# A trunk layer with sparse attention on one core: the column sums, the query norm, the gated convolution and some top-k rounds stand at other places

## The chip, the cores and the metric

One core of one Trainium2 chip. The metric is the device time of one launch in microseconds; a launch computes the whole layer once. All arithmetic is in float32 or in products split into float32r parts.

## What is computed

```python
x = x + 0.5 * swiglu(rmsnorm(x, ffn1_norm), ffn1_w_gate, ffn1_w_up, ffn1_w_down)
h = rmsnorm(x, mix_norm)
gb, gc, xv, q, k, v, qi, ki, wi = split(h @ w_in)
u = gc * xv                                   # gated convolution, width 3, 512 channels
conv_out = gb * sum(up[:, j:j + T] * conv_w[j] for j in range(3))
q = rope_partial(rmsnorm(q, q_norm), pos, 16)  # per head of 64
k = rope_partial(rmsnorm(k, k_norm), pos, 16)
score = sum over 8 heads of relu(qi . ki) * wi # indexer; masked by chunk
sel = top_k(score, n_sel)                      # 128 keys of a stream, 68 of a running one
attn = softmax(q . k[sel] / 8) @ v[sel]
x = x + concat(conv_out, attn) @ w_out
x = x + 0.5 * swiglu(rmsnorm(x, ffn2_norm), ffn2_w_gate, ffn2_w_up, ffn2_w_down)
```

There are 640 tokens (a prompt of 512 and 8 running streams of 16 with 256 cached keys each), 1024 model columns, 2816 hidden columns, 8 query heads, 2 key heads and 8 indexer heads of 64.

## The kernel before, in words

The program is written by hand for five engines; each engine runs its own list in program order, and semaphores tie the lists. There is no scheduler: the order of the work around the change is the order of the statements.

**Split products.** PE multiplies in float32r. Every operand is a high part (`wh`, `xh`) that ScalarE copies (line 934, `mixer_hi`, `set_hi_of`) and a low rest (`wl`, `xl`) that VectorE subtracts (line 1287, `split_lo`, `mixer_lo`; line 1404, `set_rest`; line 1391, `operand_rest`). A product of a 128x128 weight tile with 640 tokens is six matmuls (lines 488, 490, 492). A *part* below is such a group of six. Raw weights come by DMA from the SP queue in units of 1 MB, two slots in turn.

**The two feed-forward stages** (`ffn(0)`, `ffn(1)`). The first unit of weights is worked in four quarters: columns 0 to 3 and 4 to 7, each with two outputs (`m`). The norm's sums of squares come beside it: ScalarE squares a tile of `x`, VectorE adds it into `sqacc` (line 1310), PE sums `sqacc` over the partitions (`column_sums`, line 499), VectorE and GpSimd make the root, VectorE writes diagonals, and PE spreads them (`broadcast_rstd`, lines 506 and 507) for ScalarE to copy into `rbc`. VectorE then scales `x` and evacuates the units (`plain_out`, `plain_hid`). After four plain units come the *sets*: a scheme of seven products in the place of eight, whose first one (`set_unit` with `first=True`) waits for `operand_rest` and `set_rest` on VectorE and for `snapshot` copies on ScalarE.

**The mixer.** Units `U_TOK` to `U_TOK + 5` make the token-major projections (queries, keys, indexer), `tok_out` copies them out. `U_CONV` to `U_CONV + 5` make the twelve outputs `proj(0)` to `proj(11)` of the convolution's gates, evacuated by VectorE's `proj_out`. `top_rounds(t, n)` does n rounds of `max` and `match_replace` on the scores of tile t (lines 1613 and 1614); tile 3 needs 16 rounds in all, 4 before the low part of `U_CONV`, 5 after it, 3 and 4 later. `weigh_sample(b)` (line 1749) weighs the indexer dots of running stream b, and between two streams VectorE squares and sums a tile of the queries (`squares_of`, lines 1573 and 1575). GpSimd makes the roots (line 1841). `head_scale` multiplies the queries with the root (line 1585) and with the gain (line 1586), `rotate` (lines 1559 to 1564) turns 16 columns of each head and signals `q_ready`. PE turns the queries (line 691) behind `q_ready`, and ScalarE copies them into `q_all`. GpSimd runs `conv(i)` (lines 1893 to 1909) as soon as `proj_out` has given it `conv_v`. Both `rotate` and `conv` read and write SBUF.

The statements of VectorE around the change:

```python
close_scores(2)
top_rounds(3, 4)
mixer_lo(U_CONV)
top_rounds(3, 5)
```

Of the kernel before, what the change touches and what calls it, by code (L numbers as in the profile page):

```python
# [27 lines left out]
P = 128  # L28
# [8 lines left out]
HD = 64  # L37
# [30 lines left out]
def trunk(nc, xt, gu1, dn1, gu2, dn2, wtok, wconv, wout, small, gains, kcache, vcache, ikcache,  # L68
          conv_past, tables, bf_tables, x_keep, y_out, k_out, v_out, ik_out, conv_out):
    with ExitStack() as ctx:  # L70
# [24 lines left out]
        sm = sb("sm", [P, 36])  # L95
# [34 lines left out]
        conv_v = spare[:, 5 * TOK:6 * TOK]  # L130
# [11 lines left out]
        conv_b = sb("conv_b", [P, TOK])  # L142
# [90 lines left out]
        head_rs_ready = sem("head_rs_ready")  # L233
        ki_ready = sem("ki_ready")
# [241 lines left out]
        def _(pe):  # L476
# [117 lines left out]
            def ffn(k):  # L594
# [4 lines left out]
                for part, (cs, m) in enumerate((cs, m) for cs in (range(0, 4), range(4, 8)) for m in range(2)):  # L599
# [332 lines left out]
        def _(act):  # L932
# [34 lines left out]
            def ffn(k):  # L967
# [176 lines left out]
            def turned_out(job, dst, n):  # L1144
# [7 lines left out]
                copy(dst, src).then_inc(bank_free[bank(job)], 1)  # L1152
# [81 lines left out]
            for t in range(TT):  # L1234
                tok_out(2, t)
            mixer_hi(U_CONV + 1)
# [11 lines left out]
            for t in range(TT):  # L1248
                turned_out(f"tq{t}", qt[:, :, t * P:(t + 1) * P] if t < 4 else qt_s, 4)
# [25 lines left out]
        def _(dve):  # L1275
# [62 lines left out]
            def ffn(k):  # L1338
# [237 lines left out]

            def mean_of_squares(n, at, ss_ready):
# [3 lines left out]
            def head_scale(z, n, at, g, rs_count):  # L1581
# [4 lines left out]
                link(dve.tensor_tensor(z, z, g.unsqueeze(1).unsqueeze(1).broadcast_to([P, TT, n, HD]), ALU.mult))  # L1586
# [34 lines left out]
            def proj_out(b):  # L1621
# [14 lines left out]
                elif part == 1:  # L1636
                    if i:
                        dve.wait_ge(conv_done, i)
                    dve.wait_ge(proj_evac, b)
                    dve.tensor_tensor(halves(conv_v[:, :]), src, halves(conv_g[:, :]), ALU.mult)\  # L1640
                        .then_inc(proj_evac, 1)
                else:
                    dve.tensor_tensor(halves(conv_b[:, :]), src, halves(rbc[:, :]), ALU.mult)\
# [56 lines left out]
            link(dve.tensor_scalar(gn[:, 0, :], gn[:, 0, :], -HD ** -0.5, None, ALU.mult))  # L1700
# [30 lines left out]
            top_rounds(3, 4)  # L1731
# [292 lines left out]
```

## Time and profile before

| | |
|---|---|
| median of 3 runs | 1237.31 us (1237.16 to 1240.55) |
| the profiled execution | 1239.92 us, of it 1238.1 us span |
| PE busy | 1202.1 us, 97% |
| VectorE busy | 806.0 us, 65% |
| ScalarE busy | 484.2 us, 39% |
| GpSimd busy | 288.4 us, 23% |
| granted TensorE clock, mean | 0.988 |

The span runs from the first to the last instruction; 1.8 us of the execution lie around it. PE holds the span nearly alone, so time is lost where PE waits and where its clock is below full. In the rows below a time in square brackets is how long the engine sat idle before the instruction, and behind it the instruction that ended the wait.

### The profile page before, as it was taken

The page shows a single profiled execution, that of the slowest core. Times are in us where ns is not written, and L with a number is a line of the kernel's source. Part 1 is how long each engine was busy: PE and PEld are TensorE (multiplying, and loading weights), DVE is VectorE, ACT ScalarE, POOL GpSimd, SP SyncE. Part 2 cuts the span into 40 slices and gives each one's busy share as a digit, 9 for nine tenths or more (in the row PEclk, how much of TensorE's full clock was granted, in tenths as well). Part 3 has the DMA queues.
Part 4 walks back from the last instruction along what each step waited for, and adds up shares of the span by engine and source line. Part 5 has one row for each costly group of instructions (what it writes and reads, how often), then busy time and mean ns, then how long its engine had stood idle before and what let it go on. Part 6 is the DMA issues. An engine that isn't in the chain of part 4 may idle for free.

```text
span 1238.1 us, 20665 instructions
## 1 busy us (share of the span) xinstructions
PE 1202.1 (97%) x7992; PEld 1156.0 (93%) x7992; DVE 806.0 (65%) x1051; ACT 484.2 (39%) x716; POOL 288.4 (23%) x217
## 2 busy tenths in 40 slices
PE   8999999999999999989899899999999999999998
PEld 7999999999999999857899679999899999999998
DVE  5898777775435452377998754678877777633433
ACT  5354444444324343341133452424444444423231
POOL 0144545450000000003663000013545454100000
PEclk8999999999999999999999899999999999999999
DMA  6112121212332233111310021420122212133222
GB/s 245 69 35 100 71 102 68 102 68 69 120 118 69 83 114 103 68 35 38 134 68 35 1 63 45 146 100 35 68 102 68 102 68 102 53 126 110 84 69 102
DMA packets 24068, 103.82 MB, mean 84 GB/s; under 512 B 3536, under 2 KB 4944, under 8 KB 16592
## 3 DMA queue, kind: packets, MB, share of 16 engines
q1 hardware_dynamic: 23136, 99.28, 22.8%
q10 hardware_dynamic: 880, 3.82, 1.0%
q8 instruction: 36, 0.59, 0.2%
q14 instruction: 16, 0.13, 0.0%
HBM read 96.99 MB, written 6.10 MB: 83 GB/s over the span
## 4 chain that ended last, share of the span: by engine, by line
PE 83%; DVE 10%; issue 3%; ACT 2%; DMA 1%; ACTq 0%; DVEq 0%
PE ps L488 13%; PE ps L490 13%; PE ps L492 13%; PE ps L526 11%; PE ps L527 11%; PE ps L528 11%; PE ps L479 2%; PE ps L481 2%; PE ps L480 2%; PE ps L691 2%; PE ps L814 1%; DVE wl L1404 1%; DVE wl L1287 1%; DVE sqacc L1310 1%; PE ps L700 1%
## 5 line engine op out<-in xcount | busy, mean ns | idle before, releaser
L934 ACT ACTIVATE wh<-raw 128x1024 fp32r<-128x1024 f32 (+3 forms) x185 | 191.7, 1036 | 398.8 <-PE ps L492 286.7
L526 PE MATMUL ps<-xs,wh 128*128 128x320 f32 x720 | 223.5, 310 | 4.9 <-DVE wl L1404 4.9
L528 PE MATMUL ps<-xs,wl 128*128 128x320 f32 x720 | 223.1, 310 | 0.0
L527 PE MATMUL ps<-xs,wh 128*128 128x320 f32 x720 | 223.1, 310 | 0.0
L1287 DVE TENSOR_TENSOR wl<-raw,wh 128x1024 fp32r<-128x1024 f32 (+2 forms) x65 | 101.4, 1560 | 178.5 <-ACT wh L934 178.4
L488 PE MATMUL ps<-xs,wh 128*128 128x320 f32 x704 | 160.5, 309 | 0.5 <-DVE xs L1473 0.5
L492 PE MATMUL ps<-xs,wl 128*128 128x320 f32 x704 | 160.4, 309 | 0.0
L490 PE MATMUL ps<-xs,wh 128*128 128x320 f32 x704 | 160.4, 309 | 0.0
L1404 DVE TENSOR_TENSOR wl<-raw,wh 128x1024 fp32r<-128x1024 f32 (+1 forms) x108 | 146.9, 1362 | 8.3 <-ACT wh L934 6.3
L488 PE MATMUL ps<-xh,wh 128*128 128x320 f32 x576 | 139.8, 325 | 7.4 <-DVE wl L1287 4.3
L526 PEld LDWEIGHTS ps<-xs,wh 128*128 128x128 f32 x720 | 135.6, 188 | 6.0 <-DVE wl L1404 5.7
L528 PEld LDWEIGHTS ps<-xs,wl 128*128 128x128 f32 x720 | 135.7, 189 | 0.0
L527 PEld LDWEIGHTS ps<-xs,wh 128*128 128x128 f32 x720 | 135.7, 188 | 0.0
L490 PE MATMUL ps<-xl,wh 128*128 128x320 f32 x576 | 133.6, 314 | 0.0
L492 PE MATMUL ps<-xh,wl 128*128 128x320 f32 x576 | 133.6, 314 | 0.0
L488 PEld LDWEIGHTS ps<-xs,wh 128*128 128x128 f32 x704 | 117.7, 188 | 0.8 <-DVE xs L1473 0.8
L492 PEld LDWEIGHTS ps<-xs,wl 128*128 128x128 f32 x704 | 117.7, 188 | 0.0
L490 PEld LDWEIGHTS ps<-xs,wh 128*128 128x128 f32 x704 | 117.7, 188 | 0.0
L488 PEld LDWEIGHTS ps<-xh,wh 128*128 128x128 f32 x576 | 96.9, 193 | 18.5 <-issue 9.7
L492 PEld LDWEIGHTS ps<-xh,wl 128*128 128x128 f32 x576 | 98.7, 192 | 0.0
L490 PEld LDWEIGHTS ps<-xl,wh 128*128 128x128 f32 x576 | 98.6, 192 | 0.0
L1861 POOL TENSOR_TENSOR raw<-raw,sums 128x512 f32<-128x512 f32 x36 | 52.1, 1447 | 180.3 <-DVE wl L1404 180.3
(202 smaller groups left out, 2001.6 us busy)
## 6 DMA issues: line engine op xcount, KB each, us to landing
raw<-gu SPq DMA_DIRECT2D x43, 1024.0 KB, 4.8
raw<-dn SPq DMA_DIRECT2D x44, 512.0 KB, 3.3
raw<-wconv SPq DMA_DIRECT2D x6, 1024.0 KB, 4.8
raw<-wout SPq DMA_DIRECT2D x4, 1024.0 KB, 4.8
raw<-wtok SPq DMA_DIRECT2D x4, 840.0 KB, 4.4
x<-xt SPq DMA_DIRECT2D x8, 320.0 KB, 3.8
x_keep<-x SPq DMA_DIRECT2D x8, 320.0 KB, 3.0
x<-x_keep SPq DMA_DIRECT2D x8, 320.0 KB, 3.7
```

The costliest lines, as they stand in the source:

```text
L479: pe.matmul(out, ah, bh, start=first, stop=False)
L480: pe.matmul(out, ah, bl, start=False, stop=False)
L488: pe.matmul(o, ah, bh[:, c], start=first, stop=False)
L490: pe.matmul(o, ah, bl[:, c], start=False, stop=False)
L492: last_mm = pe.matmul(o, al, bh[:, c], start=False, stop=last)
L526: pe.matmul(out, ah, bh, start=first, stop=False, skip_group_check=True)
L527: pe.matmul(out, ah, bl, start=False, stop=False, skip_group_check=True)
L528: return pe.matmul(out, al, bh, start=False, stop=last, skip_group_check=True)
L934: return nc.scalar.activation(out, in_, ACT.Copy, scale=scale)
L1287: dve.tensor_tensor(wl[:, slot, 0:n], raw[:, slot, 0:n], wh[:, slot, 0:n].bitcast(F32), ALU.subtract).then_inc(lo_ready, 1)
L1404: dve.tensor_tensor(ring(wl_flat, part), set_source(slot, part), ring(wh_flat, part).bitcast(F32), ALU.subtract)\
L1861: pool.tensor_tensor(a[1], a[1], s2, ALU.subtract).then_inc(sum_ready, 1)
```

## The change

- PE does the column sums and the broadcast of the norm later: in `ffn(0)` two parts later each, in `ffn(1)` the sums two parts later and the broadcast as the first thing of the second unit.
- In the first set, VectorE's low part of `set_rest(0, 0, 3)` stands ahead of `operand_rest(5)`, and ScalarE's second snapshot ahead of `operand_out(6)`.
- ScalarE squares all queries in one instruction (128x2560, into `q_all`), directly behind its last `tok_out`; VectorE only sums them.
- The query gain is applied by VectorE to the 16 rotated columns of each head alone. For the other 48 it is folded, with the factor of the softmax, into the scale of ScalarE's copy behind the turn (`qgain`; for the rotated columns it holds the factor only).
- Four of the top-k rounds of tile 3 leave the place ahead of `U_CONV`'s low part and stand one by one behind `weigh_sample` of streams 2, 4, 6 and 7.
- GpSimd's and PE's other statements, SP's list and all DMAs stay as they are; the small table of constants is three columns wider.
- The convolution has two buffers for `conv_v` and `conv_b` (the second pair is `sqacc` and `sq`), and GpSimd starts it only after `q_ready`.

```diff
@@ PE
-                    if k and part == 1:
-                        column_sums(stage)
-                    if k and part == 2:
-                        broadcast_rstd(stage)
+                        if k and part == 2 and c == 5:
+                            column_sums(stage)
...
-                    if k == 0 and c == 0:
+                    if k == 0 and c == 2:
                         column_sums(stage)
-                    if k == 0 and c == 4:
+                    if c == (6, 0)[k]:
                         broadcast_rstd(stage)
@@ ScalarE
                 set_hi_of(0, 0, 2)
+                snapshot(0, 0, 1)
                 act.wait_ge(xo_lo, 7 * k + 6)
                 operand_out(6, xt_ready, 4 * k + 3)
-                snapshot(0, 0, 1)
...
             for t in range(TT):
                 tok_out(2, t)
+            act.wait_ge(tok_evac, NJ)
+            nc.scalar.activation(q_all[:, :], zq_flat, ACT.Square).then_inc(q_squared, 1)
             mixer_hi(U_CONV + 1)
...
-                turned_out(f"tq{t}", qt[:, :, t * P:(t + 1) * P] if t < 4 else qt_s, 4)
+                turned_out(f"tq{t}", qt[:, :, t * P:(t + 1) * P] if t < 4 else qt_s, 4, scale=qgain[:, 0:1])
@@ VectorE
                 plain_hid(2)
+                set_rest(0, 0, 3)
                 operand_rest(5)
                 plain_out(3, 1)
-                set_rest(0, 0, 3)
...
+            def sum_squares(t):
+                ss = head_ss[:, 3 * TT + 8 * t:3 * TT + 8 * (t + 1)].unsqueeze(1)
+                dve.wait_ge(q_squared, 1)
+                link(dve.tensor_reduce(ss, q_all[:, 512 * t:512 * (t + 1)]
+                                       .rearrange("p (t n d) -> p t n d", t=1, n=8), AX.X, ALU.add))
...
                 link(dve.tensor_tensor(z, z, rs.broadcast_to([P, TT, n, HD]), ALU.mult))
-                link(dve.tensor_tensor(z, z, g.unsqueeze(1).unsqueeze(1).broadcast_to([P, TT, n, HD]), ALU.mult))
+                part = z[:, :, :, 0:g.shape[1]]
+                link(dve.tensor_tensor(part, part, g.unsqueeze(1).unsqueeze(1)
+                                       .broadcast_to([P, TT, n, g.shape[1]]), ALU.mult))
...
-                    if i:
-                        dve.wait_ge(conv_done, i)
+                    if i > 1:
+                        dve.wait_ge(conv_done, i - 1)
+                    elif i:
+                        dve.wait_ge(q_ready, 1)
...
-            link(dve.tensor_scalar(gn[:, 0, :], gn[:, 0, :], -HD ** -0.5, None, ALU.mult))
+            link(dve.tensor_scalar(qgain[:, :], sm[:, 36:37], sm[:, 37:38], sm[:, 38:39], ALU.mult, ALU.add))
+            link(dve.tensor_scalar(qgain[:, :], qgain[:, :], -HD ** -0.5, None, ALU.mult))
...
-            top_rounds(3, 4)
             mixer_lo(U_CONV)
...
                 weigh_sample(b)
+                if b in (2, 4, 6, 7):
+                    top_rounds(3, 1)
...
-                    squares_of(heads8, 8, 3 * TT, b - 1, 1)
+                    sum_squares(b - 1)
...
-            head_scale(heads8, 8, 3 * TT, gn[:, 0, :], 3)
+            head_scale(heads8, 8, 3 * TT, gn[:, 0, 0:2 * ROT], 3)
@@ GpSimd
+            pool.wait_ge(q_ready, 1)
             for i in range(4):
                 conv(i)
```

How the lists look now, at the three places that matter. Names in them are those of the program; `top` is `top8`.

VectorE, from the closing of the scores of tiles 3 and 2 to the low part of `U_CONV`, before (the third and fourth row stand four times in a row there):

```order
L1605 MEMSET score 64x64 [waits relu_used]
L1605 MEMSET score 64x64 [waits vector_chain]
L1613 MAX top<-score 128x8 [waits vector_chain]
L1614 MATCH_REPLACE score<-top,score 128x512 [waits vector_chain]
L1287 TENSOR_TENSOR wl<-raw,wh 128x2048 [waits hi_ready,vector_chain]
```

And now (the rounds that follow are the five that stood there before too):

```order
L1617 MEMSET score 64x64 [waits relu_used]
L1617 MEMSET score 64x64 [waits vector_chain]
L1290 TENSOR_TENSOR wl<-raw,wh 128x2048 [waits hi_ready,vector_chain]
L1625 MAX top<-score 128x8
L1626 MATCH_REPLACE score<-top,score 128x512 [waits vector_chain]
```

The low part has four rounds fewer ahead of it.

VectorE, from `weigh_sample(1)` to the squares of the query tile behind `weigh_sample(2)`, before:

```order
L1749 TENSOR_SCALAR rp<-ps,wcols 128x384 [waits bank5_full]
L1573 TENSOR_TENSOR sq<-hid 128x512
L1575 TENSOR_REDUCE head_ss<-sq 128x8 [waits vector_chain]
L1749 TENSOR_SCALAR rp<-ps,wcols 128x384 [waits dec_relu_used,bank6_full,vector_chain]
L1573 TENSOR_TENSOR sq<-hid 128x512
```

And now:

```order
L1763 TENSOR_SCALAR rp<-ps,wcols 128x384 [waits bank5_full]
L1584 TENSOR_REDUCE head_ss<-q_all 128x8 [waits q_squared]
L1763 TENSOR_SCALAR rp<-ps,wcols 128x384 [waits dec_relu_used,bank6_full,vector_chain]
L1625 MAX top<-score 128x8
L1626 MATCH_REPLACE score<-top,score 128x512 [waits vector_chain]
L1584 TENSOR_REDUCE head_ss<-q_all 128x8 [waits q_squared,vector_chain]
```

The squares are gone from every stream; a round has come in at every other one.

PE, first unit of the second feed-forward stage, before (parts between the sums and the broadcast left out):

```order
L492 MATMUL ps<-xh,wl 128x320 x2
L499 MATMUL ps<-ones,sqacc 128x1 [waits sq_added]
L499 MATMUL ps<-ones,sqacc 128x1 x4
L488 MATMUL ps<-xh,wh 128x320 [waits xl_ready,xh_ready]
L506 MATMUL ps<-sq,ones 128x512 [waits diag_ready]
L507 MATMUL ps<-sq,ones 128x128
```

And now (two parts stand ahead of the sums that stood behind them, six between sums and broadcast):

```order
L491 MATMUL ps<-xh,wh 128x320 [waits xl_ready,xh_ready]
L502 MATMUL ps<-ones,sqacc 128x1 [waits sq_added]
L502 MATMUL ps<-ones,sqacc 128x1 x4
L509 MATMUL ps<-sq,ones 128x512 [waits diag_ready,lo_ready]
L510 MATMUL ps<-sq,ones 128x128
```

The sums moved back by two parts and the broadcast by four.

## Rows read from the trace of the kernel before

**Rows 1.** The page: span, and the chain that ended last by engine.

```profile
span 1238.1 us, 20665 instructions
...
PE 83%; DVE 10%; issue 3%; ACT 2%; DMA 1%; ACTq 0%; DVEq 0%
```

**Rows 2.** Timeline of PE: start, length, instruction, idle before it and its end.

```profile
27.07 1.33 PE L499 MATMUL ps<-ones,sqacc 128*128 128x1 f32 x10 [1.35 <-DVE sqacc L1310]
...
96.23 0.54 PE L526 MATMUL ps<-xs,wh 128*128 128x320 f32 x1 [1.83 <-DVE wl L1404]
...
550.74 0.90 PE L488 MATMUL ps<-xh,wh 128*128 128x320 f32 x2 [4.30 <-DVE wl L1287]
...
608.12 4.17 PE L691 MATMUL ps<-tab,hid 128*128 128x128 f32 x20 [3.89 <-DVE hid L1564]
...
801.07 1.28 PE L499 MATMUL ps<-ones,sqacc 128*128 128x1 f32 x10 [1.53 <-DVE sqacc L1310]
```

**Rows 3.** Windows: stretch, length, busy PE, PEld, DVE, ACT, POOL, granted clock, DMA.

```profile
500.00:546.00 46.00, 44.24 (x202) 31.33 (x201) 19.83 (x34) 19.52 (x35) 0.00 (x0) 1.00 0.13 46
...
550.70:554.00 3.30, 3.27 (x13) 3.27 (x14) 3.16 (x7) 0.00 (x0) 0.00 (x0) 0.54 0.65 218
...
608.10:612.00 3.90, 3.88 (x19) 3.27 (x20) 3.83 (x5) 2.05 (x4) 0.00 (x0) 0.56 0.12 17
...
801.10:806.40 5.30, 5.30 (x28) 5.30 (x29) 3.02 (x3) 0.00 (x0) 1.18 (x1) 0.68 0.33 105
...
812.00:860.00 48.00, 48.00 (x329) 48.00 (x328) 43.44 (x37) 18.55 (x18) 13.30 (x7) 1.00 0.14 47
```

**Rows 4.** Timeline of ACT: the copy of the broadcast root in the first stage.

```profile
34.60 0.70 ACT L934 ACTIVATE rbc<-ps 128x640 f32<-128x640 f32 x1 [8.77 <-PE ps L507]
```

**Rows 5.** Timeline of DVE, 543 to 566 us: rounds, low part, squares, a stream.

```profile
543.83 0.70 DVE L1613 MAX8 top<-score 128x8 f32<-128x512 f32 x1
...
545.35 0.69 DVE L1613 MAX8 top<-score 128x8 f32<-128x512 f32 x1
...
548.39 2.29 DVE L1287 TENSOR_TENSOR wl<-raw,wh 128x2048 fp32r<-128x2048 f32 x1
...
562.05 0.68 DVE L1573 TENSOR_TENSOR sq<-hid 128x512 f32<-128x512 f32 x1
...
565.92 0.62 DVE L1749 TENSOR_SCALAR rp<-ps,wcols 128x384 f32<-128x384 f32 x1 [0.50 <-PE ps L720]
```

**Rows 6.** Timeline of ACT: the weight copy behind the last `tok_out`.

```profile
547.06 1.90 ACT L934 ACTIVATE wh<-raw 128x2048 fp32r<-128x2048 f32 x1
```

**Rows 7.** Timeline of DVE, 586 to 608 us: the chain to `q_ready`.

```profile
586.75 0.82 DVE L1640 TENSOR_TENSOR hid<-ps,hid 128x640 f32<-128x640 f32 x1
...
589.69 1.93 DVE L1585 TENSOR_TENSOR zkv<-zkv,head_rs 128x640 f32<-128x640 f32 x1
...
597.89 4.08 DVE L1586 TENSOR_TENSOR hid<-hid,gn 128x2560 f32<-128x2560 f32 x1
...
602.75 0.48 DVE L1559 TENSOR_TENSOR sqacc<-hid,tab 128x320 f32<-128x320 f32 x1
603.15 1.85 DVE L1560 TENSOR_TENSOR sqacc<-hid,tab 128x320 f32<-128x320 f32 x1
604.92 1.82 DVE L1561 TENSOR_TENSOR sq<-hid,tab 128x320 f32<-128x320 f32 x1
...
607.58 0.48 DVE L1564 TENSOR_TENSOR hid<-sq 128x320 f32<-128x320 f32 x1
```

**Rows 8.** Timeline of POOL: first and last product of `conv(0)`.

```profile
587.72 3.22 POOL L1895 TENSOR_TENSOR conv_u<-hid,rbc 128x512 f32<-128x512 f32 x1 [4.57 <-DVE hid L1640]
...
604.73 1.66 POOL L1909 TENSOR_TENSOR conv_o<-conv_o,conv_b 128x640 f32<-128x640 f32 x1
```

**Rows 9.** Timeline of DVE in the second stage: its two waits for PE.

```profile
826.30 0.83 DVE L1370 TENSOR_TENSOR hid<-ps,rbc 128x640 f32<-128x640 f32 x1 [2.12 <-PE ps L492]
...
863.19 0.49 DVE L1418 TENSOR_TENSOR hid<-ps,snap 128x320 f32<-128x320 f32 x1 [3.00 <-PE ps L528]
```

More of the change, by code:

```diff
@@ L94, in trunk @@
         rstd = sb("rstd", [P, TT])
-        sm = sb("sm", [P, 36])
+        sm = sb("sm", [P, 39])
+        qgain = sb("qgain", [P, 1])
         gn = sb("gn", [P, 3, HD])
@@ L129, in trunk @@
         conv_g = spare[:, 4 * TOK:5 * TOK]
-        conv_v = spare[:, 5 * TOK:6 * TOK]
+        conv_v0 = spare[:, 5 * TOK:6 * TOK]
         zkv = sb("zkv", [P, TT, 256])
@@ L141, in trunk @@
         rp = sb("rp", [P, 2, 512])
-        conv_b = sb("conv_b", [P, TOK])
+        conv_b0 = sb("conv_b", [P, TOK])
+        conv_v, conv_b = (conv_v0, sqacc), (conv_b0, sq)
         conv_u = sb("conv_u", [P, 2 + SEQ + NB * (NT + 2)])
@@ L233, in trunk @@
         head_rs_ready = sem("head_rs_ready")
+        q_squared = sem("q_squared")
         ki_ready = sem("ki_ready")
@@ L1142, in tok_out, with turned_out @@
                 ins.then_inc(tok_evac, 1)
-            def turned_out(job, dst, n):
+            def turned_out(job, dst, n, scale=1.0):
                 wait_bank_full(act, job)
@@ L1151, in turned_out @@
                     src = src.rearrange("p (j b t) -> p j b t", j=n, b=NB)
-                copy(dst, src).then_inc(bank_free[bank(job)], 1)
+                copy(dst, src, scale=scale).then_inc(bank_free[bank(job)], 1)
             def relu_out(t, h, n):
@@ L1636, in proj_out @@
                 elif part == 1:
-                    if i:
-                        dve.wait_ge(conv_done, i)
+                    if i > 1:
+                        dve.wait_ge(conv_done, i - 1)
+                    elif i:
+                        dve.wait_ge(q_ready, 1)
                     dve.wait_ge(proj_evac, b)
-                    dve.tensor_tensor(halves(conv_v[:, :]), src, halves(conv_g[:, :]), ALU.mult)\
+                    dve.tensor_tensor(halves(conv_v[i % 2][:, :]), src, halves(conv_g[:, :]), ALU.mult)\
                         .then_inc(proj_evac, 1)
                 else:
-                    dve.tensor_tensor(halves(conv_b[:, :]), src, halves(rbc[:, :]), ALU.mult)\
+                    dve.tensor_tensor(halves(conv_b[i % 2][:, :]), src, halves(rbc[:, :]), ALU.mult)\
                         .then_inc(proj_evac, 1)
@@ L1891, in conv @@
             def conv(i):
+                v, b = conv_v[i % 2], conv_b[i % 2]
                 link(pool.tensor_copy(u_samples[:, :, 0:2], cpast[:, i, :, :]))
                 pool.wait_ge(proj_evac, 3 * i + 2)
-                pool.tensor_tensor(conv_u[:, 2:2 + SEQ], conv_v[:, 0:SEQ], rbc[:, 0:SEQ], ALU.mult)
-                link(pool.tensor_tensor(u_samples[:, :, 2:], samples(conv_v[:, SEQ:TOK]),
+                pool.tensor_tensor(conv_u[:, 2:2 + SEQ], v[:, 0:SEQ], rbc[:, 0:SEQ], ALU.mult)
+                link(pool.tensor_tensor(u_samples[:, :, 2:], samples(v[:, SEQ:TOK]),
                                         samples(rbc[:, SEQ:TOK]), ALU.mult))
@@ L1936, in tables, with q_columns @@
     return np.concatenate([np.eye(P, dtype=np.float32), cos, sin, same_t, spread, same_b, other], axis=1)
+def q_columns():
+    turned = (np.arange(P) % HD < 2 * ROT).astype(np.float32)
+    return np.stack([1.0 - turned, turned], axis=1)
 def bf_tables():
@@ L1984, in lay_out @@
         "wout": w_o.reshape(4, P, 16 * P),
-        "small": np.concatenate([norms, conv_w], axis=1),
+        "small": np.concatenate([norms, conv_w, np.tile(gains[0], 2)[:, None], q_columns()], axis=1),
         "gains": np.broadcast_to(gains[None], (P, 3, HD)),
```

6 lines of the change are left out of this document (3 added, 3 removed).

## The prediction

> **What bounds the kernel now.** I read the page first: the chain that ended last is PE for 83% of the span and VectorE for 10% [rows 1]. So PE's list is the spine, and a change gains only where PE waits or its clock is low. The timeline of PE gives the waits. The change touches four of them: 1.35 us for the squares of the first stage's norm, 4.30 us for the low part of `U_CONV`, 3.89 us for `q_ready`, 1.53 us for the squares of the second stage; a fifth, 1.83 us in the second set, it does not touch [rows 2]. The windows show what a wait costs on top. Behind the 4.30 us wait the granted clock is 0.54 for 3.3 us, behind the 3.89 us wait 0.56 for 3.9 us, behind the 1.53 us wait 0.68 over 5.3 us [rows 3]: PE falls to the lower of its two levels, 1.2 GHz in place of 2.4, and climbs back. At full clock 329 matmuls take 48.0 us [rows 3], 0.146 each, a part of six 0.88 us.
>
> **Term 1, first stage's norm.** PE issues the last matmul of the first unit so that the next could start at about 25.6 (the wait of 1.35 counts from the end of a matmul, 0.15 later) and waits until 27.07 [rows 2]. Now two parts, 1.76 us, fill that time, so the sums start at about 27.3: PE waits for nothing, but VectorE and GpSimd get the sums no earlier than before. Behind the sums PE goes at full clock, so the broadcast, again four parts later, comes at 27.3 + 0.9 + 3.5 = 31.7; before, the wait and the slow clock had put it at 33.3, and the copy of `rbc` started at 34.60 [rows 4]. It starts at 33.0. PE itself gains more, 1.6 + 1.8 (two parts already done) = 3.4, but from `rbc` on VectorE is the chain through to the second set's wait at 96.23 [rows 2], where the order of the same instructions changes little. The moves of one low part and one snapshot take away a 1.2 us wait in the first set and hand it to the 1.83 us wait behind it, which grows. I take what VectorE gains, **-1.6**, between 0 (the wait takes all) and -3.4.
>
> **Term 2, the low part of `U_CONV`.** A round takes 1.52 us (two `max` start 1.52 apart), so four are 6.1; the low part started at 548.39 and takes 2.29 [rows 5]. It now starts at 542.3 and ends at 544.6, while PE is busy until 546.4. The wait of 4.3 is gone, and the slow clock behind it: 3.3 x (1 - 0.54) = 1.5. PE begins the samples 5.9 earlier. Is VectorE there? Rounds, then key squares: five rounds from 544.6 end at 552.2, key squares at 554.0; PE brings the first sample's dots at about 554.2. It just fits. Among the samples VectorE waited 0.50 us per stream for PE and squared for 0.68 [rows 5], so 1.2 us per stream, 2.4 per two streams, are free, and a round every second stream costs 1.5. Only between streams 6 and 7 stand a round and a low part together, 3.8 us; this holds PE up by about 0.3. ScalarE's square: a copy of 2048 columns takes 1.90 [rows 6], 2560 make 2.4, done at 549.5 and read at 556; the weight copy behind it is needed 20 us later. It costs nothing, with 6 us of cover. The two tiny `qgain` operations fall into waits of VectorE. **-5.5**, between -3 (VectorE is late at the first sample, the clock stays low) and -5.9.
>
> **Term 3, `q_ready`.** VectorE's chain ran from `proj_out(1)` at 586.75 to the end of `rotate` at 608.06, 21.3 us [rows 7]. It starts 5.7 earlier, 581.0. Out go: the gain on 2560 columns, 4.08, for one on 640, nearest row 0.82 [rows 7], -3.2; and GpSimd, which waits for `q_ready` now. Beside its operations the root's product on the keys took 1.93 where the like takes 0.82, and two products of the rotation 1.85 and 1.82 where the first took 0.48 [rows 7]: -1.1 and -2.7, with 0.4 in a smaller one -4.2. That leaves 13.9: `q_ready` at 594.9 in place of 608.06. PE finishes `proj(4)` at 604.1 - 5.5 = 598.6, so it arrives last, with 3.7 us to spare. The wait of 3.89 goes. The turns took 3.9 at clock 0.56 [rows 3]; at full clock two banks and ScalarE's copies of 0.6 set them, about 2.8: -1.1. **-5.0**, between -3.9 (turns no faster) and -5.6. Of the relief by GpSimd nothing is needed: without it `q_ready` comes at 599.1 and costs 0.5.
>
> Behind it: VectorE is 13 us ahead of before, PE 10.5; three and four rounds, the mask and the evacuations ended before when PE did not yet need them, and still do. `conv(0)` now runs from 594.9; before it took from 587.72 to 606.39, 18.7 us [rows 8]. The second buffer lets `proj_out(4)` pass without `conv(0)`'s end. PE takes up the converted output over 70 us later.
>
> **Term 4, second stage's norm.** PE waited until 801.07, 1.53 us by the record [rows 2] and 1.7 counted from where the next matmul could have started, 799.4. Two parts take 1.76: the sums start at 801.1 as before, without a wait. Gone are the 1.7, the slow clock 5.3 x (1 - 0.68) = 1.7, and some 0.3 of the sums at low clock. The broadcast moves behind four more parts, which at full clock puts it where it was, 807.3; so VectorE's chain starts no earlier, PE is 3.7 ahead. VectorE had waited 2.12 and 3.00 for PE further on [rows 9], 5.1 in all, so it can follow by 3.7. **-3.7**, between -1.7 and -4.
>
> **Sum**: -1.6 - 5.5 - 5.0 - 3.7 = -15.8. Against the profiled execution, 1239.9 (span 1238.1 and 1.8 around it), 1224.1; against the median of the runs, 1237.3, which lies 2.6 under it, **1221.5**.
>
> **Rivals.**
>
> *The clock is lost anyway (12%).* The slow stretches may come from the thinner work ahead of them, not from the waits: then 1.5 + 1.1 + 1.7 of the terms stay unpaid, and the time is 1221.5 + 4.3 = 1225.8. Against it: from 500 to 546, where PE works in pieces with short waits between, the clock is 1.00 [rows 3]. The Trainium skill (TensorE: Matmul & The Clock Gate, "A second HAM failure mode: psum-queue depth-cycling") says that small idles between groups of matmuls can be enough to make the clock swing; by that rule this rival would hold. The row just named speaks against it here.
>
> *VectorE becomes the bound around the sets (13%).* In both stages the low part now stands ahead of another operand's rest, and VectorE starts no earlier in the second. If a set then waits as long as was won, terms 1 and 4 give 1 in place of 5.3: 1225.8. For it: VectorE is the chain up to 96.23. Against: the 5.1 us of waiting in rows 9.
>
> *Given back in the attention (8%).* If VectorE or ScalarE, not PE, sets the pace in the 40 items, half of 10.5 comes back: 1227. Against: both are earlier by as much as PE.
>
> *GpSimd's queue (3%), the one on the slow side.* `conv(0)` to `conv(3)` stand behind `q_ready` in one list, and PE's `w_out` parts need the last at about 674. If VectorE's work keeps GpSimd off SBUF, the end of `conv(3)` decides from 594.9 on: break-even is (674 + 15.8 - 594.9) / 4 = 24 us for each, against 18.7 in the contested `conv(0)` [rows 8]. At 27 us each the last ends at 703, and the time is 1221.5 + 29 = 1250. By the Trainium skill (SBUF — State Buffer, "SBUF: two separate sides") an operation of VectorE with two SBUF inputs and one of GpSimd lock each other out for their whole length; the rounds read one input, so that the rule too gives them no part in it.
>
> *The change does not do what it says (4%)*: VectorE's long products were not GpSimd's doing, and GpSimd delays nothing. Then the 0.5 of term 3: 1222.
>
> **How the numbers follow.** My case has 60%, the rivals 40 together. Within my case the bounds give 1218.5 to 1224.5. The range takes in the clock, the sets and part of the attention: 1217.5 to 1227.5. A measurement of this kernel tells 0.3%, 3.7 us, from nothing. Faster by more than that is every case but GpSimd's and unknown ones: 0.94. Same: 0.03. Slower: 0.03.
>
> **What would show it.** PE: no wait ahead of the first part of `proj(0)`, none ahead of the query turns, granted clock 1.00 in both places; none ahead of either column sum. `q_ready` some 13 us earlier than 608 and before PE ends `proj(4)`. VectorE's rotation products all at 0.48. The wait in the second set of the first stage grows to 2.5 to 3 us. PE's second-stage broadcast about 12 us earlier than before, its first set 16. Wrong would be: a new wait of PE at the first sample or stream 7 of over 0.5 us; a wait of VectorE on `q_squared`; a wait of over 1 us for the convolution.

## The result and the profile after

| | kernel before | changed kernel |
|---|---|---|
| median, us (range, runs) | 1237.24 (1235.85 to 1240.55, 4) | 1224.33 (1222.20 to 1224.75, 4) |
| ratio, 95% interval | 1 | 0.9888 (0.9866 to 0.9911) |
| the profiled execution | 1239.92, span 1238.1 | 1224.75, span 1222.9 |
| granted clock of PE, mean | 0.988 | 0.996 |

The changed kernel is 12.9 us faster by the medians and 15.2 by the two spans. The forecast was 1221.5 (range 1217.5 to 1227.5) for the median and a gain of 15.8 on the span. Why the two differences differ is the more interesting half of this case. One execution of the kernel before (2677.39 us) and one of `best` (2342.5 us) took about twice as long as the others and are left out of the ratios and spans below.

The page of the changed kernel, span and chain (the view of [rows 1]):

```profile
span 1222.9 us, 20664 instructions
...
PE 86%; DVE 8%; issue 3%; ACT 2%; DMA 1%; ACTq 0%; DVEq 0%
```

Timeline of PE at the places of [rows 2]: start, length, instruction, and the idle time ahead with what ended it.

```profile
27.08 1.28 PE L502 MATMUL ps<-ones,sqacc 128*128 128x1 f32 x10 [0.57 <-DVE sqacc L1313]
...
80.74 0.42 PE L529 MATMUL ps<-xr,wh 128*128 128x320 f32 x1 [1.44 <-DVE wl L1407]
...
94.81 0.42 PE L529 MATMUL ps<-xs,wh 128*128 128x320 f32 x1 [1.81 <-DVE wl L1407]
...
544.50 0.45 PE L491 MATMUL ps<-xh,wh 128*128 128x320 f32 x2
...
596.62 1.04 PE L692 MATMUL ps<-tab,hid 128*128 128x128 f32 x8
598.00 1.24 PE L692 MATMUL ps<-tab,hid 128*128 128x128 f32 x8 [0.34 <-ACT q_all L935]
599.44 0.66 PE L692 MATMUL ps<-tab,hid 128*128 128x128 f32 x4 [0.20 <-ACT q_all L935]
599.85 0.54 PE L491 MATMUL ps<-xh,wh 128*128 128x320 f32 x2
...
789.20 1.22 PE L502 MATMUL ps<-ones,sqacc 128*128 128x1 f32 x10
790.28 0.54 PE L491 MATMUL ps<-xh,wh 128*128 128x320 f32 x2
```

`proj(0)` (544.50), the query turns (596.62) and the second stage's column sums (789.20) start with no bracket behind them: three waits of 4.30, 3.89 and 1.53 us are gone. Two shorter ones of 0.34 and 0.20 inside the turns are ScalarE's copies. Ahead of the first stage's sums (27.08) a wait of 0.57 is left, where the prediction had none.

Windows of the changed kernel (stretch, length, busy PE, PEld, DVE, ACT, POOL, granted clock, DMA share, GB/s), the places of [rows 3]:

```profile
544.00:551.00 7.00, 7.00 (x48) 6.88 (x48) 6.67 (x15) 4.84 (x3) 0.00 (x0) 1.00 0.42 153
...
596.60:600.50 3.90, 3.36 (x26) 2.72 (x25) 3.76 (x8) 2.90 (x5) 3.60 (x8) 1.00 0.63 250
...
789.20:794.00 4.80, 4.80 (x37) 4.80 (x36) 2.99 (x3) 0.00 (x0) 1.18 (x1) 1.00 0.27 77
```

The granted clock, 0.54 to 0.68 at these places before, is 1.00. VectorE's chain to `q_ready` (the view of [rows 7]), and the first of the rounds behind it:

```profile
579.30 0.82 DVE L1654 TENSOR_TENSOR hid<-ps,hid 128x640 f32<-128x640 f32 x1
...
588.71 0.82 DVE L1597 TENSOR_TENSOR hid<-hid,gn 128x640 f32<-128x640 f32 x1
...
590.70 0.49 DVE L1563 TENSOR_TENSOR sqacc<-hid,tab 128x320 f32<-128x320 f32 x1
591.11 0.48 DVE L1564 TENSOR_TENSOR sq<-hid,tab 128x320 f32<-128x320 f32 x1
...
592.44 0.49 DVE L1567 TENSOR_TENSOR hid<-sq 128x320 f32<-128x320 f32 x1
...
595.04 0.69 DVE L1625 MAX8 top<-score 128x8 f32<-128x512 f32 x1
```

And GpSimd, which now waits for `q_ready` (the view of [rows 8]):

```profile
592.99 2.19 POOL L1910 COPY conv_u<-cpast 128x16 f32<-128x16 f32 x1 [16.18 <-DVE hid L1567]
595.26 1.30 POOL L1912 TENSOR_TENSOR conv_u<-hid,rbc 128x512 f32<-128x512 f32 x1
...
604.13 1.57 POOL L1926 TENSOR_TENSOR conv_o<-conv_o,conv_b 128x640 f32<-128x640 f32 x1
```

`q_ready` comes at 592.93 in place of 608.06, 3.7 us before PE asks for it. The chain takes 13.6 us (forecast 13.9, before 21.3), and `conv(0)` 12.7 in place of 18.7: each engine is faster without the other's products beside it.

Where PE won time, by the starts of the same matmuls in both traces: 1.7 at the indexer dots (526.25 to 524.51), 10.5 from there to `proj(5)` (612.05 to 599.85), 0.3 given back from there to the second stage's sums (most of it the attention), 3.3 behind them. Together 15.2.

### The profile page after: what moved, and what is told of

Its sections match the earlier page's. It is cut to its first block, busy times and chain, and to the rows that moved or that the text cites. A ratio compares the mean times of both kernels' runs of the same rounds, so it can differ in the third digit from the quotient of the medians.

```text
span 1222.9 us, 20664 instructions
## 1 busy us (share of the span) xinstructions
PE 1194.9 (98%) x7992; PEld 1148.9 (94%) x7992; DVE 795.7 (65%) x1047; ACT 487.1 (40%) x717; POOL 281.8 (23%) x217
## 4 chain that ended last, share of the span: by engine, by line
PE 86%; DVE 8%; issue 3%; ACT 2%; DMA 1%; ACTq 0%; DVEq 0%
PE ps L491 14%; PE ps L495 13%; PE ps L493 13%; PE ps L529 11%; PE ps L531 11%; PE ps L530 11%; PE ps L482 2%; PE ps L484 2%; PE ps L483 2%; PE ps L692 1%; PE ps L815 1%; DVE wl L1407 1%; PE ps L701 1%; PE ps L775 1%; ACT xh L935 1%
## 5 line engine op out<-in xcount | busy, mean ns | idle before, releaser
L491 PEld LDWEIGHTS ps<-xh,wh 128*128 128x128 f32 x576 | 94.8, 189 | 14.3 <-issue 10.1
L529 PE MATMUL ps<-xr,wh 128*128 128x320 f32 x288 | 89.7, 311 | 3.4 <-DVE quart L1421 1.6
```

The source lines that it names most:

```text
L491: pe.matmul(o, ah, bh[:, c], start=first, stop=False)
L529: pe.matmul(out, ah, bh, start=first, stop=False, skip_group_check=True)
```

## The experiments

Each kernel was profiled and timed beside the kernel before. The trace of each gives four distances of PE. The work between the points is the same in all kernels, with two exceptions: the unread products of the two fill kernels, and the two parts (1.76 us) that stand ahead of the second stage's sums where the norm is moved. Those two parts fill the wait ahead of the sums, so the third distance keeps its length and the last one gets shorter:

| kernel | median us | ratio to before (95%) | start to dots | dots to query turns | turns to 2nd-stage sums | sums to end | clock |
|---|---|---|---|---|---|---|---|
| before | 1237.3 | | 523.9 | 84.3 | 193.0 | 437.0 | 0.988 |
| again_before | 1237.01 | 0.9997 (0.9983, 1.0011) | 524.9 | 85.1 | 191.9 | 438.6 | 0.987 |
| norm_only | 1233.72 | 0.9969 (0.9958, 0.9981) | 522.1 | 84.4 | 190.2 | 433.7 | 0.994 |
| mixer_only | 1229.08 | 0.9929 (0.9914, 0.9944) | 523.6 | 74.5 | 190.9 | 437.1 | 0.993 |
| changed | 1224.33 | 0.9888 (0.9866, 0.9911) | 522.1 | 74.5 | 192.6 | 433.7 | 0.996 |
| again_after | 1223.39 | 0.9892 (0.9877, 0.9907) | 522.2 | 74.5 | 188.0 | 433.8 | 1.000 |
| rounds_only | 1235.05 | 0.9985 (0.9970, 1.0001) | 524.6 | 79.6 | 189.9 | 437.0 | 0.993 |
| squares_back | 1225.18 | 0.9900 (0.9884, 0.9916) | 522.6 | 75.6 | 192.6 | 433.8 | 0.994 |
| conv_early | 1226.26 | 0.9919 (0.9894, 0.9945) | 522.4 | 76.6 | 192.1 | 434.2 | 0.993 |
| one_buffer | 1222.56 | 0.9875 (0.9850, 0.9900) | 522.2 | 74.5 | 188.9 | 433.8 | 0.999 |
| set_order_back | 1224.90 | 0.9892 (0.9866, 0.9917) | 523.3 | 74.5 | 190.9 | 434.3 | 0.992 |
| fill_waits2 | 1238.94 | 1.0000 (0.9987, 1.0014) | 523.5 | 84.1 | 192.3 | 437.0 | 0.992 |
| fill_less | 1236.38 | 0.9984 (0.9966, 1.0001) | 523.9 | 82.9 | 189.1 | 437.1 | 0.994 |
| best | 1220.92 | 0.9867 (0.9842, 0.9893) | 520.9 | 74.2 | 189.5 | 434.0 | 0.997 |

(Dots: the first indexer dots of token tile 3. Clock: mean granted clock of the profiled execution.) The first distance is 523.5 to 524.9 in the six kernels without the moved norm, and 522.1 to 522.6 in six of the eight with it (the other two are `set_order_back` and `best`). The second and fourth hardly change unless a kernel changes them: 74.5 in five traces, 437.0 or 437.1 in five of six.

The third, mostly the attention, runs over 188.0 to 193.0 in no relation to the change. What it follows is the clock. Windows of the changed kernel, then of again_after, the same program:

```profile
670.00:740.00 70.00, 62.00 (x463) 49.91 (x463) 41.98 (x124) 34.03 (x97) 0.00 (x0) 0.93 0.14 43
```

```profile
670.00:740.00 70.00, 61.57 (x493) 50.12 (x493) 43.24 (x129) 36.10 (x105) 0.00 (x0) 1.00 0.14 43
```

PE's waits from 600 to 784 us are the same in both (4.7, 2.1, 1.8 and 0.3 us), and the distance is 192.6 and 188.0. In all fourteen traces it goes by the clock of this window: 188.0 and 188.9 us at 1.00, 189.1 to 190.2 at 0.98, 190.9 to 192.1 at 0.95, 192.3 to 193.0 at 0.93. Whole spans of two kernels can therefore differ by up to 5 us for this alone.

### The same kernels again: what an execution adds

> The kernel before, run again, to see how much one profiled execution of it says. Theory A (each long wait of PE is always paid twice, once as wait and once as slow clock): the second profile has the same four waits, 1.35, 4.30, 3.89 and 1.53 us, and the same granted clock behind them, 0.54, 0.56 and 0.68, and a span of 1237 to 1239. Theory B (the waits are fixed, but whether and how long the clock falls behind a wait differs from execution to execution): the waits are the same within 0.1 us, the clock behind at least one of them is above 0.9 or below by another length, the mean clock differs by 0.002 or more from 0.988, and the executions spread over 3 us or more. Theory B would explain why the medians lie 12.9 us apart and the two spans 15.2.

> The changed kernel again, on the same chip as the three above. Theory A: 1222 to 1225, its gain the sum of the two halves within 1 us. Theory B: its executions spread less than those of before (2 us or less), because the long waits behind which the clock falls are gone.

The three later waits are the same in both executions of the kernel before (4.30 and 4.35, 3.89 twice, 1.53 twice). The one ahead of the first sums is not, 1.35 and 2.42: PE comes earlier, since its clock from 8.5 to 20 us is 0.85 in the one and 1.00 in the other. Waits of PE between 545 and 615 us in again_before (total, times, longest), the same figures as in the kernel before:

```profile
PE ps L488 <- DVE wl L1287: 4.3, 1, 4.3
PE ps L691 <- DVE hid L1564: 3.9, 1, 3.9
```

The clock behind them is not. Windows of the kernel before, then of again_before, right behind the wait of 4.3 us:

```profile
551.00:560.00 9.00, 9.00 (x56) 8.67 (x57) 8.59 (x18) 0.00 (x0) 0.00 (x0) 0.85 0.33 118
```

```profile
551.00:560.00 9.00, 8.27 (x41) 8.27 (x42) 8.66 (x17) 0.00 (x0) 0.00 (x0) 0.68 0.33 118
```

56 matmuls against 41 in the same 9 us, for the same program (in again_before PE still waits in the first 0.7 of them). So how long the clock stays low belongs to an execution, not to the program alone. That it falls behind these waits belongs to the program, as far as the traces go: behind the wait of 4.3 us in all three traces that have it, behind 3.9 in all four, behind 1.53 in all six. Behind the wait of 1.8 us in the second set of the first stage it fell in five of twelve (0.72 to 0.76 from 96 to 102 us, 1.00 in the other seven), and in the attention in twelve of fourteen.

Over 70 executions of the kernel before, those with a mean clock of 0.993 have spans of 1233.1 to 1233.4 us and those at 0.987 reach 1240.5. The nine of the changed kernel run from 0.992 (span 1225.0) to 1.000 (1218.4). The means are 0.990 and 0.996. The shortest spans, 1233.1 and 1218.4, lie 14.7 apart.

Of the expectations, Theory B held for the kernel before, but for the first wait and for the mean clock (0.987, only 0.001 from 0.988). For the changed kernel it failed: its five executions spread over 6.5 us, not 2 or less, so the waits that are gone are not all that makes the executions differ.

### The two halves

norm_only is the kernel before with the moves of the column sums, the broadcasts and the order in the sets; mixer_only is the changed kernel without them. Part of norm_only's edit (left out are the later broadcast, the first stage's sums and the orders in the first set, all as in the change):

```diff
-                    if k and part == 1:
-                        column_sums(stage)
-                    if k and part == 2:
-                        broadcast_rstd(stage)
...
+                        if k and part == 2 and c == 5:
+                            column_sums(stage)
```

> Before, with only the moves of the column sums, the broadcasts and the order in the first set; the mixer as before. Theory A (terms add): against before -1.6 to the second set of the first stage and -3.4 to -3.7 in the second stage, 5.1 us in all, 1232 where before has 1237.2; no wait at the second stage's column sums. Rival (the sets give it back): less than 2.5 us. In the mixer the waits of 4.3 and 3.9 us stand as before.

> The changed kernel with the column sums, the broadcasts and the order in the first set put back as before. Theory A: -10.1 us against before by the trace (PE's first part of the second feed-forward stage about 10 us earlier than in before), 1227 where before has 1237.2; the waits of 1.35 and 1.53 us at the column sums are back. Theory B: the medians give less than that by up to 2 us, 1229. Rival (what is won in the mixer is given back in the attention): less than 6 us.

Against the kernel before on the same chip (median 1237.39) the halves are worth 3.7 and 8.3 us, together 12.0 against the changed kernel's 14.0. The forecasts were 5.1 and 10.1 (by the medians up to 2 less), with a sum that meets the whole within 1 us. By the medians norm_only gave less than forecast, and the sum misses the whole by 2 us. In the table each half does its part alone, and there they add: norm_only shortens the first and the last distance by 1.8 and 3.3, mixer_only the second by 9.8, and the changed kernel the same three by 1.7, 3.3 and 9.8.

### The rounds alone

The kernel before, with four rounds moved between the streams and nothing else. (The expectation speaks of five rounds and 5.5 us; the edit moves four, 6.1 us.)

```diff
-            top_rounds(3, 4)
             mixer_lo(U_CONV)
...
                 weigh_sample(b)
+                if b in (2, 4, 6, 7):
+                    top_rounds(3, 1)
```

> The kernel before, with the five top-k rounds moved out from ahead of the low part of U_CONV to behind sample streams 2, 4, 6 and 7; nothing of VectorE's query work, of GpSimd's convolution or of the norms is changed. Theory: the wait of 4.3 us ahead of proj(0) goes (the rounds took 5.5 us there, and the low part of U_CONV is then done before TensorE asks for it), but the rounds come back as 5.5 us of VectorE's work between the sample streams, where the changed kernel had made room by giving the query squares to ScalarE. So q_ready on VectorE comes at most some 1 us earlier than in the kernel before (608.06 us), while TensorE is 5.7 us earlier at it: the wait ahead of the query turns grows from 3.9 to some 8 or 9 us and gives nearly all of the gain back. Time: 0 to -1.5 us against the kernel before. Rival (VectorE has slack between the samples that absorbs the rounds): q_ready is 4 us earlier or more, the wait stays at 4 us, and the time is 4 to 5.5 us below the kernel before.

Waits of PE in rounds_only, on the timeline:

```profile
574.29 0.91 PE L720 MATMUL ps<-rp,tab 128*128 128x384 f32 x2 [1.27 <-DVE rp L1748]
...
604.19 4.17 PE L691 MATMUL ps<-tab,hid 128*128 128x128 f32 x20 [3.91 <-DVE hid L1564]
```

The theory on record failed and its rival held in the trace: the wait for `q_ready` did not grow, it stayed at 3.91, since VectorE had slack between the streams and moved up with PE (`q_ready` at 604.13 in place of 608.06). The distance from dots to turns fell by 4.6 us (84.3 to 79.6). One wait of 1.27 us at the last stream is new. The median fell only by 2.3 us, not the rival's 4 to 5.5, and its interval touches 1: the mean clock of its 12 executions is 0.989, no better than before.

### Parts of the query work undone

squares_back gives the squares back to VectorE between the streams; conv_early takes GpSimd's wait for `q_ready` out; one_buffer uses a single pair of buffers for the convolution.

```diff
-            nc.scalar.activation(q_all[:, :], zq_flat, ACT.Square).then_inc(q_squared, 1)
...
-                    sum_squares(b - 1)
+                    squares_of(heads8, 8, 3 * TT, b - 1, 1)
```

> The changed kernel with the query squares back on VectorE, eight heads of one tile between the sample streams as in the kernel before (ScalarE's one instruction of 2.35 us gone); all else as changed. Theory: ScalarE's square took about 2.2 us of work off VectorE between streams; with it back VectorE falls behind in the streams with both a round and a squares piece, its waits there (0.55, 1.07 and 1.07 us) are used up first, and q_ready moves from 592.9 to 594.5 to 595.5, still ahead of the 596.6 at which TensorE asks. Some short waits of TensorE on rp of the order of 0.2 to 1 us in all. Time +0.5 to +2 us against the changed kernel. Rival (the squares on ScalarE are what makes the moved rounds affordable): q_ready is later than TensorE, a wait of 2 us or more comes back ahead of the query turns, +3 us or more.

```profile
572.37 0.91 PE L721 MATMUL ps<-rp,tab 128*128 128x384 f32 x2 [1.29 <-DVE rp L1761]
```

The wait that rounds_only showed is back (0.22 in the changed kernel), `q_ready` comes at 594.50, the distance is 1.1 us longer, and no wait comes back at the turns, as the theory had it. Having the squares on ScalarE is worth 1.1 us in the trace; by the medians it cannot be told from nothing.

```diff
-            pool.wait_ge(q_ready, 1)
             for i in range(4):
```

> The changed kernel without GpSimd's wait for q_ready ahead of conv(0): the convolution runs beside VectorE's gain and rotation again. Theory: contention between the two engines comes back, a rotation product takes some 1.8 us instead of 0.49 or conv(0) takes 18 us instead of 12.7, and q_ready moves from 592.9 to about 597, just behind TensorE's 596.6: +0.5 to +1 us against the changed kernel. Rival (the shortened gain and the squares on ScalarE are what brings q_ready forward, and the neighbour costs little): products at 0.5 to 0.7 us, q_ready under 594.5, time 0.

Timeline of VectorE and of PE in conv_early:

```profile
590.76 2.08 DVE L1597 TENSOR_TENSOR hid<-hid,gn 128x640 f32<-128x640 f32 x1
...
594.02 1.87 DVE L1563 TENSOR_TENSOR sqacc<-hid,tab 128x320 f32<-128x320 f32 x1
595.81 1.85 DVE L1564 TENSOR_TENSOR sq<-hid,tab 128x320 f32<-128x320 f32 x1
```

```profile
599.05 1.09 PE L692 MATMUL ps<-tab,hid 128*128 128x128 f32 x8 [1.95 <-DVE hid L1567]
```

Three products lengthen by 1.26, 1.38 and 1.37 us, `q_ready` comes at 598.99, and PE waits 1.95 us. The prediction had 599.1 and a price of 0.5. That the time came out is luck: the chain from 579.62 takes 19.4 us, 5.7 more than the changed kernel's where the prediction had 4.2 (it had left out the shortened gain product, which takes 2.08 beside GpSimd and not 0.82); but it also starts 1.4 earlier than the 581.0 assumed. The price was too low because PE asked at about 597.0 (599.05 less the wait), not 598.6. The median is 2 us above the changed kernel's, with intervals that overlap. The Trainium skill (SBUF — State Buffer, "SBUF: two separate sides") has an operation of VectorE with two SBUF inputs and one of GpSimd that reads SBUF lock each other out. The traces agree: 0.49 alone and 1.87 beside GpSimd; and the `max` at 595.04, with one input, keeps its 0.69 beside GpSimd's product at 595.26.

```diff
-        conv_v, conv_b = (conv_v0, sqacc), (conv_b0, sq)
+        conv_v, conv_b = (conv_v0, conv_v0), (conv_b0, conv_b0)
...
                     if i:
-                        dve.wait_ge(q_ready, 1)
+                        dve.wait_ge(conv_done, i)
```

> The changed kernel with a single pair of buffers for the convolution, so that VectorE's evacuation of each next part waits for GpSimd's convolution of the one before, as in the kernel before. Theory: proj_out(4) stood at 599.6; it now waits for the end of conv(0), which starts behind q_ready and ends at about 605.7, 6 us later; what VectorE has behind it (mask, logits' low parts) moves by up to 6 us, TensorE's next evacuation waits appear as 1 to 3 us near 600 to 625: +1 to +3 us. Rival (the stage behind has the slack): 0 to +0.5 us.

```profile
605.91 0.83 DVE L1652 TENSOR_TENSOR hid<-ps,hid 128x640 f32<-128x640 f32 x1 [6.32 <-POOL conv_o L1924]
```

The theory (1 to 3 us) failed. VectorE does wait 6.32 us for GpSimd, but of it only one wait of 0.9 us reaches PE in the attention (at 634.70); the third distance is 1.0 longer than in again_after, whose clock is as high. The median, 1222.56, is not above the changed kernel's. The second buffer is worth 1.0 us in a trace at most, and no time that was measured.

### The order in the sets

```diff
                 set_hi_of(0, 0, 2)
+                snapshot(0, 0, 1)
                 act.wait_ge(xo_lo, 7 * k + 6)
                 operand_out(6, xt_ready, 4 * k + 3)
-                snapshot(0, 0, 1)
...
                 plain_hid(2)
+                set_rest(0, 0, 3)
                 operand_rest(5)
                 plain_out(3, 1)
-                set_rest(0, 0, 3)
```

> The changed kernel with the two moves in the sets undone (the snapshot ahead of the operand on ScalarE, the rest of the set ahead of the operand on VectorE, as in the kernel before); the norm's sums and broadcast stay where the change put them. In the changed kernel the waits of TensorE on the stage's weights between 60 and 110 us are 5.3 us in six pieces, in the kernel before 3.0 in two, with the start 1.4 us earlier. Theory (VectorE's chain from rbc on sets the end of the second set, the order only deals the waits out): the second set ends within 0.3 us of the changed kernel's, time 0 to +0.5 us. Rival (the moves are what lets TensorE through): the wait of 1.8 at the last piece grows to 3 or more and the time by 1 to 1.5 us.

PE and VectorE in set_order_back, and a window of its granted clock:

```profile
80.16 0.63 PE L529 MATMUL ps<-xs,wh 128*128 128x320 f32 x1 [2.97 <-DVE wl L1407]
```

```profile
83.76 0.49 DVE L1421 TENSOR_TENSOR hid<-ps,snap 128x320 f32<-128x320 f32 x1 [1.25 <-PE ps L531]
...
94.92 1.22 DVE L1407 TENSOR_TENSOR wl<-raw,wh 128x1024 fp32r<-128x1024 f32 x1
```

```profile
78.00:84.00 6.00, 3.84 (x14) 3.84 (x15) 4.75 (x7) 4.45 (x7) 0.00 (x0) 0.61 0.29 93
```

PE is now further ahead of VectorE than in the kernel before, and with the old order it waits 2.97 us in the first set at one place; behind it the clock is 0.61, PE's result for the snapshot is late, VectorE waits 1.25 us for it, and its low part starts at 94.92. In the changed kernel PE waits less in the first set, in three pieces of 0.21, 1.44 and 0.18 us, the clock stays at 1.00, and the low part starts at 93.54. The dots come 1.2 us later with the old order. So the theory (the second set ends within 0.3 us) failed, and the rival had the size right and the place wrong: the wait at the last piece shrank to 0.75. The clock from 78 to 84 us is 1.00 in all thirteen other traces. The median (1224.90) is too near for a verdict, and the trace is one execution: whether the clock would fall there each time is open.

### Filling the two waits

The kernel before with products that nobody reads in PE's two long waits, first 23 and 21 of them, then 17 and 15:

```diff
             tok_unit(2, 1, range(3, TT))
+            wait_bank_read(pe, "wcol")
+            for _ in range(17):
+                pe.matmul(ps[:, 6, 0:P], ones[:, :], ones[:, :], start=True, stop=True)
             proj(0)
```

> The kernel before with work that nobody reads put into TensorE's two long waits: 23 products of 128x128 ahead of proj(0) and 21 ahead of the wait for q_ready (0.166 us each by the 32 like it at the kernel's start: 3.8 and 3.5 us inside waits of 4.3 and 3.9). Nothing that VectorE or ScalarE does moves, so proj(0) and the query turns start when they did. Theory B (a wait costs its own time and, in some executions, also a stretch at the lower clock behind it): the starts stay within 0.3 us, the granted clock is 1.00 behind both places in the profiled execution (before: 0.85 and 0.72 in the windows there), and the median is 1.5 to 3.5 us below the kernel before. Theory A (the low-clock stretches have nothing to do with the waits): low clock still shows behind one of the two, and the time is that of the kernel before within 0.5 us.

> The kernel before with unread products in TensorE's two long waits again, but fewer: 17 ahead of proj(0) and 15 ahead of the wait for q_ready, since in the trace of fill_waits2 a product took 0.217 us (46 halves from 545.9 to 550.9), not 0.166, and both groups ran 0.6 us past the end of the wait. Now they take 3.7 of 4.3 us and 3.3 of 3.9. Theory B (the lower clock behind the two places came from the waits and costs TensorE time): the distance from the last indexer dots' start to the first query turn is 84.2 - 1.5 (or less; the stretch at 608 lies in the turns, behind it) = 82.5 to 83 us; granted clock 1.00 in both places; median 1 to 3 us below the kernel before. Theory A' (what fill_waits2 showed: the clock lost behind one place turns up at another, in the attention, so that filling waits wins nothing): granted clock 1.00 in both places, but the mean over the execution stays at 0.990 to 0.992 and the median within 0.7 us of the kernel before.

Timeline of PE in fill_less at both places, and its window behind the first:

```profile
550.78 0.56 PE L488 MATMUL ps<-xh,wh 128*128 128x320 f32 x2 [0.51 <-DVE wl L1293]
...
606.83 1.09 PE L691 MATMUL ps<-tab,hid 128*128 128x128 f32 x8 [0.56 <-DVE hid L1570]
```

```profile
551.00:560.00 9.00, 9.00 (x72) 8.55 (x71) 8.59 (x18) 0.00 (x0) 0.00 (x0) 1.00 0.33 117
```

In both kernels, one trace each, the clock is 1.00 behind both places, where it fell in every trace that has the waits. So the low clock there did come from the waits. From `proj(0)` to the first sample takes 7.2 us in place of 8.6 or 9.5. That is the clock's price at that place, 1.4 to 2.3 us, apart from the wait's own time; the turns take 3.1 in place of 3.9, another 0.8. fill_waits2 spent its gain on products that ran 0.6 us over the end of each wait. Its median was expected 1.5 to 3.5 us below the kernel before and is 1.6 above (1237.35 beside it), the ratio is 1.0000: nothing was won. fill_less shortens dots to turns by 1.3, and its median is 1.0 us lower with an interval that touches 1. Why so little of the clock's gain shows in the medians is open. That it is lost again at another place is not shown: the low clock at 680 us in fill_less's trace (0.83 from 680 to 690) is there in the kernel before too (0.67).

### A version that does a little more

```diff
-                    if c == (6, 0)[k]:
+                    if c == (5, 0)[k]:
...
-                if b in (2, 4, 6, 7):
+                if b in (2, 4, 5, 7):
```

> The changed kernel with two small moves more: the first broadcast one part earlier (behind part 5 of ffn(0), not 6), which brings rbc and VectorE's chain to the second set 0.9 us forward, and the top-k round behind stream 6 moved behind stream 5, away from the low part of the weights between streams 6 and 7, which takes away TensorE's wait of 0.2 us there. Expected: the second set ends 0.9 us earlier, -1.0 us against the changed kernel in all. Rival (squares of the last tiles or ScalarE's root are not ready a part earlier, so TensorE waits at the broadcast): a new wait of 0.3 to 0.9 us at the broadcast and a time equal to the changed kernel's.

```profile
93.78 0.41 PE L529 MATMUL ps<-xs,wh 128*128 128x320 f32 x1 [1.81 <-DVE wl L1407]
```

The second set's wait ends 1.03 us earlier, the dots come 1.2 earlier and the wait of 0.22 between the streams is gone. The median is 1220.92 us, 3.1 below the nine executions of the changed kernel (1223.97, on other chips), the lowest of this study; but the intervals against the kernel before overlap, and its one trace vouches for 1.5 of it (0.3 less if the last distance, 434.0, is counted). The rival, a new wait at the broadcast, did not appear.

## Why the prediction was right, and where it was not

- **Term 1, first stage's norm, forecast -1.6.** Measured -1.4 at the second set's wait, -1.7 at the dots. The mechanism held: the sums start at 27.08 as before, the rest follows at full clock (`rbc` is copied at 33.09, forecast 33.0). One step failed: "where the order of the same instructions changes little". In set_order_back, one trace, the gain is lost at the second set without the moves (96.19, against 94.81 with them and 96.23 before). And the wait of 1.83 did not grow to 2.5 to 3 us (it is 1.81): PE's waits in the sets from 60 to 110 us grew from 3.0 to 5.3 us in all, but in short pieces around it.
- **Term 2, the low part of `U_CONV`, forecast -5.5.** From the dots to the first sample 6.0 us went: the wait, and the slow clock behind it. One wait of 0.22 us in the streams gives a little back (forecast about 0.3). rounds_only shows the mechanism by itself in the trace, with 4.6 us by the turns. None of the signs of being wrong appeared: no wait of over 0.5 us at the first sample or stream 7, and between 540 and 700 us none of VectorE's waits that last is for the squares or for the convolution.
- **Term 3, `q_ready`, forecast -5.0.** About -4.7, with `q_ready` 2.0 us earlier than forecast, since VectorE began at 579.3. The relief by GpSimd was 5.7 and not 4.2 (conv_early), and it was needed: without it PE waits 1.95 us. The turns take 3.2 in place of 3.9 (forecast 2.8): ScalarE's copies with the gain as scale take 0.68 us, not 0.60, and PE waits 0.54 for them.
- **Term 4, second stage's norm, forecast -3.7.** The last distance fell by 3.3 in both kernels with the move; the broadcast comes 11.7 us earlier (forecast about 12) and the first set 15.2 (about 16). The term was 0.3 to 0.4 too large because the sums were taken as 0.8 us at full clock and last 1.08 (789.20 to 790.28).
- **The rivals.** GpSimd's queue: `conv(0)` and `conv(1)` take 12.7 us each, far from the break-even of 24. VectorE around the sets: held off, by the order. Attention: 0.3 given back between two traces that both had a clock of 0.93 there. The clock: 1.00 at the three places shown.
- **The sum's base.** The sum of 15.8 met the spans (15.2) better than the medians (12.9). Against the profiled execution's time it gave 1224.1, and the changed kernel's profiled execution took 1224.75. But that agreement is in part luck, since the two executions had the same low clock in the attention: the second pair of traces of the same two kernels, again_before and again_after, differs by 22.1 us. What the traces give place by place, 1.7, 10.5 and 3.3, is sound and close to the terms. The step to the median is the weak one. The profiled execution of the kernel before lay 2.6 us above its median, that of the changed kernel 0.4 above, and this is the whole difference between 15.2 and 12.9. The prediction took all of its clock terms from one execution and did not ask how far executions of one kernel spread (spans of 1233.1 to 1240.7 us for the kernel before). No execution at the median was profiled, so which low-clock stretch it lacks is open. The stretches behind the waits are unlikely to be it, since every trace with those waits had them.

Shown by experiments: the two halves, and that they add in the traces (by the medians 12.0 against 14.0); the slack of the streams; what squares, convolution and buffers are worth in a trace; that the two waits bring the low clock behind them. Only argued or open: what the order in the sets does for the clock, why the filled waits gain so little, and why the low-clock stretches of the attention come and go.

## What to carry to other kernels

Price a wait and the slow clock behind it apart: here the wait of 4.3 us was the same in two executions within 0.05 us, and the clock behind it cost 1.4 in the one and 2.3 in the other. Compare two traces place by place and not by their spans, since low clock at places that the change doesn't touch moves a span by several us. Keeping VectorE's two-input products and GpSimd's work apart paid on both engines. And where an earlier start lengthens one wait, look at the order of the work on the engine behind it: in the sets another order brought the dots forward by 1.2 us.

## Not expected of the hardware

- The same program, with the same wait of 4.3 us to 0.05 us, had granted clocks of 0.85 and 0.68 in the same 9 us behind it.
- The clock fell behind a wait of 1.53 us in six traces of six, and behind one of 1.8 us, in the second set of the first stage, in five of twelve.
- The five float32 products with one column each, the column sums, hold PE for 1.08 us at full clock in ten instructions, some 0.22 each. A product with 128 columns takes the same 0.22 (fill_waits2: 23 products in 46 instructions from 545.85 to 550.90).
- GpSimd's first small copy of `conv(0)` (128x16) took 2.19 us behind VectorE's product of 2.29 that began 0.15 earlier; the like takes 0.20 elsewhere.
